# A two-layer transformer trunk on one core: down weights of the experts asked for from a second queue, tokens in residue order, gate product first

## The chip, the core and the metric

One NeuronCore of a Trainium2 chip runs the whole program. Its engines are TensorE (PE in the profile; PEld is its weight load), VectorE (DVE), ScalarE (ACT), GpSimd (POOL) and SyncE (SP). Each has its own instruction stream and they wait for each other on semaphores. Sixteen DMA engines move data between HBM and the on-chip memory (SBUF); here SP and GpSimd ask for transfers, each on its own queue. Products are accumulated in PSUM, which has 8 banks of 128 x 512 floats. The metric is the time of one execution on the device, in microseconds (us).

## What is computed

256 tokens of width 1024 go through two layers. Each layer has four token mixers in parallel, a feed-forward part (dense in layer 0, top-2 of 8 experts in layer 1), and a gated input embedding.

```python
def dilated_attention(q, k, v, window, dilation):      # mixer C: (128, 1), (512, 4), (2048, 16)
    # positions t = u*d + c are split into d residue classes, each a sliding window
    o, lse = banded_attention(to_classes(q), to_classes(k), to_classes(v), window // (2 * dilation), C_BLOCK, None)
...
    merged = merged + gates[:, :, n] * (o.reshape(bsz, seq, BRANCH_WIDTH) @ w_branch[n])
...
def swiglu(h, wg, wu, wd):
    return (jax.nn.silu(h @ wg) * (h @ wu)) @ wd
# layer 1: every token goes to 2 of 8 experts, each with wg, wu (1024 x 3584) and wd (3584 x 1024)
    h = rms_norm(x, ffn_pre_g[i]); x = x + rms_norm(f, ffn_post_g[i])
    e = (p[i] @ ple_w_proj[i]) * sigmoid(x @ ple_w_gate[i]); x = x + rms_norm(e, ple_post_g[i])
```

All arrays are float32, and the eight experts' weights are 352 MB of the 507 MB that are read.

## The kernel before

Tokens lie as two tiles of 128: token `t*128 + p` is in partition p of tile t. All large weights pass through `ring`, six slots of 1 MB each. SP asks for them in the order of `ring_plan()`; before a slot is filled again SP waits for the semaphore that tells that its last contents are used (`released`, `expert_load`). A wait on SP holds back everything behind it on SP.

Precise products are made of three rounded ones. ACT casts a weight slot to a rounded copy (`expert_his`, L1370 and L1373, "hi"), DVE subtracts that from the slot (`expert_los`, L1809 and L1814, "lo"), and PE multiplies hi by hi, hi by lo and lo by hi.

**The experts.** `expert_chunk` is written once for each engine and runs 56 times, for 8 experts of 7 chunks of 512 hidden columns. A chunk b uses six loads: slots 0 and 1 (two halves of the up weights), 2 and 3 (gate), 4 and 5 (down). PE's order in a chunk is: up product with slot 0; the transposition of the hidden values of chunk b-1 (`expert_turn`, L983, here called the turn); up product with slot 1; the down product of chunk b-1 (L964, slots 4 and 5); gate products with slots 2 and 3 (all of them L1022). In one chunk of each expert PE also gathers the next expert's tokens (L974), and in another it scatters the last expert's result (L1003). ACT's order is: casts of slots 0 and 1 of b, cast of slot 4 of b-1, silu of b-1 (L1378), cast of slot 5 of b-1, cast of the turned hidden values (L1382), casts of slots 2 and 3, and a copy of the up product out of PSUM (L1432). DVE's is: splits of slots 0 and 1 of b, split of slot 4 of b-1, the multiplication of silu by up (`expert_hidden`, L1821), split of slot 5 of b-1, split of the turned values (L1825), splits of slots 2 and 3. Slots 0 to 3 come free when PE has used them (`up_gate_used`), 4 and 5 when DVE has split them (`down_split`). SP asks in the order 0 and 1 of b, 4 and 5 of b-1, 2 and 3 of b. The rows of up and gate weights in a slot are 2 KB long, those of down weights 4 KB.

**The mixers.** `MIXER` is one list of steps that each engine follows. PE does for each head: two `fill` units (L1170, L1177), `turn` (transposed probabilities, L1140), `score` of the next head (L909) and `pv` (L1153). Mixer C, the last of the four, has three sets of scores in a head, one for each pair of window and dilation, all 256 keys wide, in banks 4 and 5; the third one follows `pv`. One exponential runs over all sets together.

**The start.** SP asks for x in two tiles, a small table, four weight loads and then the tables (1.5 MB). DVE waits for both tiles of x, and splits the first weights after the first tile of x is transposed.

Of the kernel before, what the change touches and what calls it, by code (L numbers as in the profile page):

```python
# [27 lines left out]
ALU = mybir.AluOpType  # L28
# [35 lines left out]
                ("mask", 4 * NT * SEQ), ("full", 2 * NT * HD), ("axial", 2 * NT * HD), ("rope_a", 2 * NT * A_ROPE))  # L64
# [4 lines left out]
CONST_W = _n  # L69


def constants():
# [12 lines left out]
    q = (np.arange(NT)[None, :] * P + p[:, None])[:, :, None]  # L85
    k = np.arange(SEQ)[None, None, :]
    masks = []
    for window, dil in PATTERNS:
        masks.append((q % dil == k % dil) & (np.abs(q - k) <= window // 2))
    masks.append(np.abs(q - k) <= D_HALF_WINDOW)  # L90
# [9 lines left out]
    pos = np.arange(NT)[None, :] * P + p[:, None]  # L100
# [52 lines left out]
NSETS = {"A": 1, "B": 1, "C": 3, "D": 1}  # L153
# [113 lines left out]
class ExpertPass:  # L267
# [3 lines left out]
    def __init__(self, sem, tag, slots, loads0):  # L271
# [4 lines left out]
        self.up_copied, self.silu_ready = sem(f"{tag}_up_copied"), sem(f"{tag}_silu_ready")  # L276
# [69 lines left out]
def trunk(nc, args):  # L346
# [5 lines left out]
    with ctx:  # L352
# [44 lines left out]
        peak = sb("peak", [P, 2, NT, 3])  # L397
# [21 lines left out]
        probs = take(2 * NT * 3 * SEQ).rearrange("p (j t g s) -> p j t g s", j=2, t=NT, g=3)  # L419
# [32 lines left out]
        e_hidden, e_silu, e_up = hidden[:, 0:ECW], silu[:, 0:ECW], silu[:, ECW:2 * ECW]  # L452
# [38 lines left out]
        UP_BANK, TURN_BANK, GATE_BANK, SPREAD_BANK = (ps[:, b, :] for b in range(4))  # L491
# [10 lines left out]
        mask = const("mask", 4 * NT * SEQ).rearrange("p (m t s) -> p m t s", m=4, t=NT)  # L502
# [4 lines left out]

        const_in_s, x_in_s = sem("const_loaded"), [sem(f"x{t}_loaded") for t in range(NT)]
# [27 lines left out]
        main_pass = ExpertPass(sem, "moe", slot_in, [(LOOPS[1] + j) // RING for j in range(RING)])  # L536
# [27 lines left out]
        def loaded(eng, pos):  # L564

            eng.wait_ge(slot_in[pos % RING], 16 * (pos // RING + 1))
# [22 lines left out]
        def _(sp):  # L589
# [74 lines left out]
            def all_expert_loads(run):  # L664

                def chunk(b, e, c, before):
                    for j in (0, 1):
                        expert_load(run, j, b, e, c)
                    if before:
                        for j in (4, 5):  # L670
                            expert_load(run, j, b - 1, *before)
# [3 lines left out]
                for j in range(RING):  # L675
                    expert_load(run, j, 0, 0, 0)
# [7 lines left out]
                for j in (4, 5):  # L684
                    expert_load(run, j, ALL_CHUNKS - 1, N_EXPERTS - 1, E_CHUNKS - 1)
# [5 lines left out]
            expert_views = [moe_view(moe_w_up[0]), moe_view(moe_w_gate[0]),  # L691
                            moe_w_down[0].rearrange("e (c h k p) d -> e c h p k d", h=2, k=2, p=P)]

            x_v, first = x_in[0].rearrange("(t p) d -> p t d", p=P), CONST_AT["upper"]
# [1383 lines left out]
```

## Time and profile before

| | before |
|---|---|
| median of 3 runs | 2068.84 us (2068.57 to 2075.63) |
| the profiled execution | 2068.97 us, of which the span is 2067.2 us |
| PE busy, PEld busy | 1985.2 us (96%), 1677.5 us (81%) |
| DVE, ACT, POOL busy | 1355.1 us, 1106.8 us, 58.6 us |
| bytes by SP's queue, by GpSimd's | 497.92 MB, 7.91 MB |
| experts (first gather to last scatter) | 997.55 to 2015.6 us of the span |

The span is what the profiler sees of the program. Times within it count from its start. PE is busy nearly always, but a busy PE says little on a whole, since its ends are modelled; the distance between the starts of its groups is the better measure. The page's DMA row for the experts shows 324 to 374 GB/s in each slice, against 102 to 194 in most of the rest.

### The profile page before, as it was taken

The numbers are of one execution on the slowest core, as the hardware profiler recorded it, in microseconds if no ns is written. First come the engines' busy times: TensorE is split into PE (matmuls) and PEld (weight loads), VectorE is DVE, ScalarE is ACT, GpSimd is POOL, SyncE is SP. The second block draws the span as 40 slices with busy tenths as digits, with TensorE's granted clock in tenths as the row PEclk, the third lists the DMA queues.
The fourth block names the chain that finished last, engine by engine and source line by source line (L and its number), as shares of the span: only waits on it lengthen the run. The fifth ranks groups of instructions, "written<-read, shape, count | busy, mean of one in ns | idle before, by whom it ended". The sixth has DMA issues, their size and how long they took to land.

```text
span 2067.2 us, 27265 instructions
## 1 busy us (share of the span) xinstructions
PE 1985.2 (96%) x10126; PEld 1677.5 (81%) x10126; DVE 1355.1 (66%) x1504; ACT 1106.8 (54%) x1174; POOL 58.6 (3%) x104
## 2 busy tenths in 40 slices
PE   6999998999998999999799999999999999999986
PEld 5888887999986888887688888878888888888864
DVE  3345345555546424435588888888888888888864
ACT  4233334333335333333477776777777777777743
POOL 2100002000001100000000000000000000000000
PEclk9999999999999999999799999999999999999998
DMA  8533336555535533323599998999999999998970
GB/s 299 163 102 103 102 122 190 188 187 187 188 133 194 189 118 102 123 91 132 220 368 342 353 372 325 374 331 354 359 338 374 338 356 350 351 373 324 374 288 28
DMA packets 253345, 506.70 MB, mean 245 GB/s; under 512 B 8304, under 2 KB 90384, under 8 KB 253152
## 3 DMA queue, kind: packets, MB, share of 16 engines
q1 hardware_dynamic: 250592, 497.92, 67.1%
q0 software_dynamic: 2688, 7.91, 1.3%
q8 instruction: 42, 0.69, 0.1%
q14 instruction: 23, 0.19, 0.0%
HBM read 504.75 MB, written 1.05 MB: 245 GB/s over the span
## 4 chain that ended last, share of the span: by engine, by line
PE 89%; DVE 3%; ACT 3%; DMA 2%; issue 2%; SPq 0%; POOL 0%; DVEq 0%; ACTq 0%; POOLq 0%
PE ps L1022 27%; PE ps L964 19%; PE ps L1170 11%; PE ps L934 9%; PE ps L866 4%; PE ps L1109 4%; PE ps L1177 3%; PE ps L909 2%; PE ps L844 2%; PE ps L974 2%; PE ps L1153 1%; DMA ring<-in_w_in_dram 1%; PE ps L983 1%; PE ps L1140 1%; ACT down_hi_w L1373 1%
## 5 line engine op out<-in xcount | busy, mean ns | idle before, releaser
L1809 DVE TENSOR_TENSOR ring_lo<-ring,up_gate_hi_w 128x2048 fp32r<-128x2048 f32 x224 | 504.4, 2289 | 62.5 <-ACT up_gate_hi_w L1370 61.6
L1370 ACT CAST up_gate_hi_w<-ring 128x2048 fp32r<-128x2048 f32 x224 | 423.5, 1914 | 86.3 <-DMA ring<-in_moe_w_up_dram 82.5
L1022 PE MATMUL ps<-up_gate_hi_w,tokens_hi 128*128 128x512 f32 x896 | 355.1, 396 | 1.3 <-DVE ring_lo L1809 1.3
L1022 PE MATMUL ps<-up_gate_hi_w,tokens_lo 128*128 128x512 f32 x896 | 349.5, 390 | 0.0
L1022 PE MATMUL ps<-ring_lo,tokens_hi 128*128 128x512 f32 x896 | 349.0, 389 | 0.0
L1814 DVE TENSOR_TENSOR down_lo_w<-ring,down_hi_w 128x2048 fp32r<-128x2048 f32 x112 | 256.6, 2291 | 56.8 <-ACT down_hi_w L1373 56.4
L1170 PE MATMUL ps<-hT,ring 128*128 128x256 f32 x1024 | 231.7, 379 | 0.0
L1373 ACT CAST down_hi_w<-ring 128x2048 fp32r<-128x2048 f32 x112 | 214.1, 1912 | 25.2 <-DMA ring<-in_moe_w_down_dram 24.2
L1170 PEld LDWEIGHTS ps<-hT,ring 128*128 128x128 f32 x1024 | 193.5, 190 | 26.1 <-issue 0.3
L1022 PEld LDWEIGHTS ps<-up_gate_hi_w,tokens_lo 128*128 128x128 f32 x896 | 168.2, 188 | 35.9
L1022 PEld LDWEIGHTS ps<-up_gate_hi_w,tokens_hi 128*128 128x128 f32 x896 | 168.3, 188 | 35.2 <-issue 1.7
L1022 PEld LDWEIGHTS ps<-ring_lo,tokens_hi 128*128 128x128 f32 x896 | 168.4, 188 | 33.2
L964 PE MATMUL ps<-down_hi_w,hidden_hi 128*128 128x512 f32 x576 | 181.7, 397 | 3.4 <-DVE hidden_lo L1825 3.3
L964 PE MATMUL ps<-down_lo_w,hidden_hi 128*128 128x512 f32 x576 | 179.0, 392 | 0.0
L964 PE MATMUL ps<-down_hi_w,hidden_lo 128*128 128x512 f32 x576 | 178.2, 391 | 0.0
L934 PE MATMUL ps<-hT_hi,up_gate_hi_w 128*128 128x256 f32 x512 | 146.0, 285 | 1.4 <-DVE hT_lo L1630 1.4
L934 PE MATMUL ps<-hT_hi,ring_lo 128*128 128x256 f32 x512 | 145.9, 285 | 0.0
L934 PE MATMUL ps<-hT_lo,up_gate_hi_w 128*128 128x256 f32 x512 | 145.9, 285 | 0.0
L964 PEld LDWEIGHTS ps<-down_lo_w,hidden_hi 128*128 128x128 f32 x576 | 108.7, 189 | 23.6
L964 PEld LDWEIGHTS ps<-down_hi_w,hidden_lo 128*128 128x128 f32 x576 | 108.6, 189 | 23.5
L964 PEld LDWEIGHTS ps<-down_hi_w,hidden_hi 128*128 128x128 f32 x576 | 103.3, 189 | 29.3 <-issue 8.3
L1517 ACT ACTIVATE egate<-ps 128x256 f32<-128x256 f32 x64 | 24.6, 385 | 179.0 <-PE ps L1177 179.0
(218 smaller groups left out, 2661.0 us busy)
## 6 DMA issues: line engine op xcount, KB each, us to landing
ring<-in_moe_w_up_dram SPq DMA_DIRECT2D x112, 1024.0 KB, 5.0
ring<-in_moe_w_gate_dram SPq DMA_DIRECT2D x112, 1024.0 KB, 5.0
ring<-in_moe_w_down_dram SPq DMA_DIRECT2D x112, 1024.0 KB, 8.6
ring<-in_w_in_dram SPq DMA_DIRECT2D x58, 1024.0 KB, 5.2
ring<-in_ffn_w_up_dram SPq DMA_DIRECT2D x16, 1024.0 KB, 5.3
ring<-in_ffn_w_gate_dram SPq DMA_DIRECT2D x16, 1024.0 KB, 7.9
ring<-in_ffn_w_down_dram SPq DMA_DIRECT2D x16, 1024.0 KB, 9.6
ring<-in_w_branch_dram SPq DMA_DIRECT2D x8, 1024.0 KB, 4.9
```

Source lines behind the costliest of these rows:

```text
L844: m = mm(bank[:, 0:w], a[:, 4 * half + k, t * P:(t + 1) * P], b[:, k, 0:w], start=(half == k == n == 0), stop=(half == 1 and k == 3 and n ...
L866: m = mm(acc(t)[:, half, :], a[:, 2 * i + k, t * P:(t + 1) * P], w[:, k, half * 512:(half + 1) * 512], start=(i == k == n == 0), stop=(i = ...
L934: m = mm(ps[:, j, i * SEQ:(i + 1) * SEQ], w[:, k, cols], xs[:, k, :], start=(k == 0 and n == 0), stop=(k == NK - 1 and n == 2))
L964: m = mm(to(t)[:, half, :], a[:, j, t * P:(t + 1) * P], w[:, j % 2, half * 512:(half + 1) * 512], start=first and n == 0, stop=last and n ...
L1022: m = mm(bank, xs[:, 4 * half + k, :], w[:, k, :], start=(half == k == n == 0), stop=(half == 1 and k == 3 and n == 2))
L1109: m = mm(bank[:, t * SEQ:(t + 1) * SEQ], hT[:, k, t * P:(t + 1) * P], wv[:, k, :], start=(k == 0), stop=(k == NK - 1))
L1170: mm(bank[:, 0:SEQ], wg[:, k, (c % 2) * P:(c % 2 + 1) * P], hT[:, k, :], start=(k == 0), stop=(k == NK - 1))
L1177: m = mm(bank[:, SEQ:2 * SEQ], wb[:, k, c * P:(c + 1) * P], oT[:, 2 * n + k, :], start=(k == 0), stop=(k == 1))
L1370: copy(up_gate_hi_w[:, j, :], ring[:, slot, :]).then_inc(run.up_gate_hi, 1)
L1373: copy(down_hi_w[:, j - 4, :], ring[:, slot, :]).then_inc(run.down_hi, 1)
L1809: v.tensor_tensor(ring_lo[:, slot, :], ring[:, slot, :], up_gate_hi_w[:, j, :], ALU.subtract)\
L1814: v.tensor_tensor(down_lo_w[:, j - 4, :], ring[:, slot, :], down_hi_w[:, j - 4, :], ALU.subtract)\
```

## The change

It has four parts.

1. **Down weights on GpSimd's queue.** In the experts of layer 1 slots 4 and 5 are asked for by GpSimd (`down_load`), which waits on `down_split` itself; SP asks only for slots 0 to 3. These two slots get semaphores of their own.
2. **Gate first.** The gate weights take slots 0 and 1 and the up weights 2 and 3. ACT makes silu at the end of its chunk, the copy of the up product is gone, and DVE multiplies straight out of PSUM.
3. **Residue order.** Token `4*(p % 64) + 2*t + p // 64` is in partition p of tile t, so that tokens of one tile agree mod 4 only with tokens of the same tile. In mixer C the sets for dilation 4 and 16 need the keys of their own tile alone and share one set: NSETS of C goes from 3 to 2. x, p and the output are moved in halves of 64 partitions, and the mask table is 256 KB smaller.
4. **Early weights.** At the start the first weight load stands ahead of the second tile of x, ACT casts and DVE splits it before the second tile's work, and the tables have their own semaphore.

```diff
+            def down_load(j, e, c):
+                slot = expert_slot(j)
+                dst = ring[:, slot, :].rearrange("p (k c) -> p k c", k=2)
+                pool.dma_start(dst, down_view[e][c][j % 2]).then_inc(main_pass.slots[slot], 16)
...
+                if layer % 2:
...
+                    with pool.Fori(1, N_EXPERTS) as e:
+                        with pool.Fori(0, E_CHUNKS) as chunk:
+                            for j in (4, 5):
+                                pool.wait_ge(main_pass.down_split, 2 * (e * E_CHUNKS + chunk - 1) + j - 3)
+                                down_load(j, e, chunk)
...
-                    if before:
+                    if before and run is over_pass:
                         for j in (4, 5):
                             expert_load(run, j, b - 1, *before)
...
-                    wait_from(pe, run.up_copied, b)
-                    product(UP_BANK, 0)
+                    wait_from(pe, run.silu_ready, b)
+                    product(GATE_BANK, 0)
...
-                    product(GATE_BANK, 2)
-                    product(GATE_BANK, 3)
+                    wait_from(pe, run.hidden_ready, b)
+                    product(UP_BANK, 2)
+                    product(UP_BANK, 3)
...
-                act.wait_ge(run.up_gate_used, 4 * b + 4)
+                act.wait_ge(run.up_gate_used, 4 * b + 2)
...
-                dve.wait_ge(run.up_copied, b + 1)
+                dve.wait_ge(run.up_gate_used, 4 * b + 4)
                 wait_from(dve, run.turned, b)
-                v.tensor_tensor(e_hidden, e_silu, e_up, ALU.mult).then_inc(run.hidden_ready, 1)
+                v.tensor_tensor(e_hidden, e_silu, UP_BANK, ALU.mult).then_inc(run.hidden_ready, 1)
...
+                    if g == 0:
+                        q, k = score_operands(b, h, 0)
+                        m = mm(bank[:, t * SEQ:(t + 1) * SEQ], q[:, tile], k, start=True, stop=True)
+                        continue
+                    for i in range(2):
+                        q, k = score_operands(b, h, 1 + i)
+                        m = mm(bank[:, t * SEQ + i * P:t * SEQ + (i + 1) * P], q[:, tile], k[:, tile], start=True, stop=True)
...
-                    for t in range(NT):
-                        act.wait_ge(x_in_s[t], 16)
-                        square((layer, "pre", t), x[:, t, :], junk)
+                    act.wait_ge(x_in_s[0], 32)
+                    square((layer, "pre", 0), x[:, 0, :], junk)
+                    z_his(layer, 0, 0)
                     tile_his(layer, "pre", 0)
```

The loads of a later chunk on SP, in the loop over the chunks of the first expert. Before, `ring` is filled with up, up, down, down, gate, gate, and the down loads stand behind the wait for the second up slot:

```order
L662 ISA [waits moe_up_gate_used]
L662 DMA ring<-in_moe_w_up_dram 128x4x512
L657 REGISTER_ALU
L662 ISA [waits moe_up_gate_used]
L662 DMA ring<-in_moe_w_up_dram 128x4x512
L659 ISA
L662 ISA [waits moe_down_split]
L662 DMA ring<-in_moe_w_down_dram 128x2x1024
L659 REGISTER_ALU
L662 ISA [waits moe_down_split]
L662 DMA ring<-in_moe_w_down_dram 128x2x1024
```

The same loop after, on SP; gate stands where up stood, and no down load is left:

```order
L673 ISA [waits moe_up_gate_used]
L673 DMA ring<-in_moe_w_gate_dram 128x4x512
L668 REGISTER_ALU
L673 ISA [waits moe_up_gate_used]
L673 DMA ring<-in_moe_w_gate_dram 128x4x512
L668 REGISTER_ALU
L673 DMA ring<-in_moe_w_up_dram 128x4x512 [waits moe_up_gate_used]
L668 REGISTER_ALU
L673 DMA ring<-in_moe_w_up_dram 128x4x512 [waits moe_up_gate_used]
```

And on GpSimd, where after the load of p nothing but the down loads stands until the experts are done:

```order
L827 DMA work<-in_p_dram 64x2x256 [waits residual_ready,mix_ready]
L827 DMA work<-in_p_dram 64x2x256
L786 DMA ring<-in_moe_w_down_dram 128x2x1024 [waits mix_ready] x2
L832 UNCONDITIONAL_BRANCH
L832 ISA
L786 ISA [waits moe_down_split]
L786 DMA ring<-in_moe_w_down_dram 128x2x1024
L834 REGISTER_ALU
L786 ISA [waits moe_down_split]
L786 DMA ring<-in_moe_w_down_dram 128x2x1024
```

What moved: a down load no longer stands behind a wait for PE on its queue; it is asked for as soon as DVE has split the slot.

PE in the mixer C of layer 0 before, one head, from its fill units (L1170, L1177) over the transposed probabilities (L1140), scores (L909) and the products with v (L1153):

```order
L1170 MATMUL ps<-hT,ring 128x256 x8
L1177 MATMUL ps<-work,ring 128x256 x2
L1140 MATMUL ps<-cn,work 128x128 x12
L909 MATMUL ps<-work 128x256 x4
L1153 MATMUL ps<-work 64x128 x12
L909 MATMUL ps<-work 128x256 x2
```

The same head after (L1207 and L1214 are the fill units, L1180 the transpositions, L949 and L953 the scores, L1194 the products with v):

```order
L1207 MATMUL ps<-hT,ring 128x256 x8
L1214 MATMUL ps<-work,ring 128x256 x2
L1180 MATMUL ps<-cn,work 128x128 x8
L949 MATMUL ps<-work 128x256 x2
L953 MATMUL ps<-work 128x128 x4
L1194 MATMUL ps<-work 64x128 x8
```

Four transpositions and four products with v are gone; four wide score products became four of 128 columns, and none stands behind the products with v any more.

## Rows read from the trace of the kernel before

**Rows 1.** The page: shares of the chain that ended last.

```profile
PE 89%; DVE 3%; ACT 3%; DMA 2%; issue 2%; SPq 0%; POOL 0%; DVEq 0%; ACTq 0%; POOLq 0%
```

**Rows 2.** Stretches of time: length, busy time and count by engine, PE clock, DMA share, GB/s.

```profile
990.00:1000.00 10.00, 4.75 (x21) 4.65 (x22) 8.27 (x28) 0.38 (x2) 0.00 (x0) 0.50 0.07 29
...
1015.00:1020.00 5.00, 3.12 (x13) 2.17 (x12) 4.46 (x3) 4.97 (x4) 0.00 (x0) 1.00 0.93 352
...
1065.00:1082.00 17.00, 17.00 (x78) 13.95 (x77) 15.61 (x9) 12.97 (x10) 0.00 (x0) 1.00 1.02 375
```

**Rows 3.** PE's timeline, a head of mixer C: start, duration, engine, line, tiles, count.

```profile
244.04 1.47 PE L1140 MATMUL ps<-cn,work 128*128 128x128 f32 x12
245.35 1.89 PE L909 MATMUL ps<-work 128*128 128x256 f32 x8
247.17 1.53 PE L1153 MATMUL ps<-work 128*64 128x128 f32 x24
248.63 1.13 PE L909 MATMUL ps<-work 128*128 128x256 f32 x4
249.60 0.59 PE L1170 MATMUL ps<-hT,ring 128*128 128x256 f32 x2
```

**Rows 4.** The same timeline, two heads with one set.

```profile
183.37 1.03 PE L909 MATMUL ps<-work 128*128 128x256 f32 x4
184.32 0.66 PE L1153 MATMUL ps<-work 128*64 128x128 f32 x8
...
217.55 0.66 PE L1153 MATMUL ps<-work 128*64 128x128 f32 x8 [0.67 <-ACT work L1504]
```

**Rows 5.** The chain in order of time: the gather of 16 products with 128 columns.

```profile
1235.60 3.57 PE ps L974 x32
```

**Rows 6.** Timelines of PE, ACT, DVE and SP, one chunk of the third expert.

```profile
1306.41 0.60 PE L983 MATMUL ps<-cn,work 128*128 128x128 f32 x4
...
1323.26 0.60 PE L983 MATMUL ps<-cn,work 128*128 128x128 f32 x4
...
1314.99 1.92 ACT L1370 CAST up_gate_hi_w<-ring 128x2048 fp32r<-128x2048 f32 x1 [1.28 <-DMA ring<-in_moe_w_up_dram]
1317.64 1.92 ACT L1373 CAST down_hi_w<-ring 128x2048 fp32r<-128x2048 f32 x1 [0.73 <-DMA ring<-in_moe_w_down_dram]
...
1302.84 2.29 DVE L1814 TENSOR_TENSOR down_lo_w<-ring,down_hi_w 128x2048 fp32r<-128x2048 f32 x1 [0.46 <-ACT down_hi_w L1373]
...
1319.70 2.29 DVE L1814 TENSOR_TENSOR down_lo_w<-ring,down_hi_w 128x2048 fp32r<-128x2048 f32 x1 [0.46 <-ACT down_hi_w L1373]
1321.91 0.68 DVE L1821 TENSOR_TENSOR work<-work 128x512 f32<-128x512 f32 x1
...
1306.81 3.51 SPq L662 DMA_DIRECT2D ring<-in_moe_w_up_dram  x2
1310.69 1.00 SPq L662 DMA_DIRECT2D ring<-in_moe_w_down_dram  x2
```

**Rows 7.** The page, DMA issues: KB each, median us from issue to landing.

```profile
ring<-in_moe_w_up_dram SPq DMA_DIRECT2D x112, 1024.0 KB, 5.0
...
ring<-in_moe_w_down_dram SPq DMA_DIRECT2D x112, 1024.0 KB, 8.6
```

**Rows 8.** DMA packets of 987 to 989 us by queue: packets, MB, share of 16 engines.

```profile
q1 hardware_dynamic: 101, 0.41, 55.4%
q0 software_dynamic: 101, 0.35, 44.0%
```

**Rows 9.** DMA packets of two stretches, 1295 to 1298 us and 1299 to 1301 us.

```profile
DMA packets 539, 1.20 MB, mean 401 GB/s; under 512 B 16, under 2 KB 16, under 8 KB 539
...
DMA packets 221, 0.84 MB, mean 420 GB/s; under 512 B 16, under 2 KB 16, under 8 KB 221
```

**Rows 10.** The chain in order of time, at the start: start, us, what.

```profile
10.10 26.26 DMA ring<-in_w_in_dram
...
40.81 11.15 PE ps L844 x48
```

**Rows 11.** PE's timeline at the end of the experts.

```profile
1996.63 0.39 PE L1022 MATMUL ps<-up_gate_hi_w,tokens_lo 128*128 128x512 f32 x1
1998.43 0.66 PE L983 MATMUL ps<-cn,work 128*128 128x128 f32 x4 [1.42 <-DVE work L1821]
2002.42 1.22 PE L964 MATMUL ps<-down_hi_w,hidden_hi 128*128 128x512 f32 x2 [3.33 <-DVE hidden_lo L1825]
```

More of the change, by code:

```diff
@@ L84, in constants @@
     put("iota8", np.broadcast_to(np.tile(np.arange(8, dtype=np.float32), NT), (P, NT * 8)))
[L85 to L90, printed above, removed]
+    pos = token_at()
+    q, k = pos[:, :, None], pos.T.reshape(1, 1, SEQ)
+    near = lambda a, b, window, dil: (a % dil == b % dil) & (np.abs(a - b) <= window // 2)
+    own = pos.T[None, :, :]
+    masks = [near(q, k, *PATTERNS[0]), np.concatenate([near(q, own, *PATTERNS[1]), near(q, own, *PATTERNS[2])], -1),
+             np.abs(q - k) <= D_HALF_WINDOW]
     put("mask", np.stack([np.where(m, 0.0, MASKED) for m in masks], 1).astype(np.float32))
@@ L451, in trunk @@
         silu = take(4 * SEQ)
-        e_hidden, e_silu, e_up = hidden[:, 0:ECW], silu[:, 0:ECW], silu[:, ECW:2 * ECW]
+        e_hidden, e_silu = hidden[:, 0:ECW], silu[:, 0:ECW]
         hidden = hidden.rearrange("p (n s) -> p n s", n=2)
@@ L673, in chunk @@
                         expert_load(run, j, b, e, c)
-                for j in range(RING):
+                for j in range(RING if run is over_pass else 4):
                     expert_load(run, j, 0, 0, 0)
@@ L701, in _ @@
                     load(pos)
+                    if pos == 0:
+                        for c in range(2):
+                            sp.dma_start(x[64 * c:64 * c + 64, 1, :], x_v[c, 1]).then_inc(x_in_s[1], 16)
                     if pos == 3:
-                        sp.dma_start(cn[:, first:], const_in[:, first:]).then_inc(const_in_s, 16)
+                        sp.dma_start(cn[:, first:], const_in[:, first:]).then_inc(tables_in, 16)
                 if layer % 2 == 0:
@@ L1128, in _ @@
                             emptied(layer, "swap", {"A": "Ak", "B": "Bk", "C": "C2k", "D": "Dk"}[b], 1 if b == "A" else 0)
-                        later = MIXER[step_number + 1][0] == "pv" and NSETS[b] == 3
-                        for g in range(2 if later else NSETS[b]):
+                        for g in range(NSETS[b]):
                             score(layer, j, b, h, g)
@@ L1150, in _ @@
                             n = SETS * layer + SET0[j] + g
-                            for kt in range(NT):
+                            for i in range(2):
                                 for t in range(NT):
-                                    m = mm(O_BANK[t * HD:(t + 1) * HD, h % 2, :], values(b, h, g, kt),
-                                           pT[:, n % NPT, kt, t * P:(t + 1) * P],
-                                           start=(g == 0 and kt == 0), stop=(g == NSETS[b] - 1 and kt == NT - 1))
+                                    v = values(b, h, 0, i) if g == 0 else values(b, h, 1 + i, t)
+                                    m = mm(O_BANK[t * HD:(t + 1) * HD, h % 2, :], v, pT[:, n % NPT, i, t * P:(t + 1) * P],
+                                           start=(g == i == 0), stop=(g == NSETS[b] - 1 and i == 1))
                             m.then_inc(pv_done, 1)
-                        before = MIXER[step_number - 1]
-                        if before[0] == "score" and NSETS[before[2]] == 3:
-                            score(layer, *before[1:], 2)
                     elif s[0] == "fill":
```

96 lines of the change are left out of this document (55 added, 41 removed).

## The prediction

> **What bounds the kernel now.** I read the chain that ended last first: PE holds 89% of it, DMA 2% [rows 1]. Then the stretches, to see whether that holds in each stage. In a middle stretch of the experts PE is busy 17.00 of 17.00 us, the clock is 1.00, and the DMA engines move 375 GB/s at a share of 1.02 [rows 2]. So PE is the bound there and the DMA engines are close behind; the reader should see both full at once. The third view is the timelines of a single chunk, because a mean can't tell how much slack a load has. The turn of a chunk starts at 1306.41 us and that of the next at 1323.26, 16.85 us later [rows 6], and it is the same in the other chunks without a gather or scatter. 56 chunks make nearly half of the span, so each 0.1 us in a chunk is 5.6 us.
>
> **Slack of a chunk's loads.** The turn can only start when DVE has multiplied silu by up. DVE does that behind its split of slot 4, which is behind its split of slot 1. The row of the split starts at 1319.70 and takes 2.29, the multiplication takes 0.68 and ends at 1322.6; the turn starts at 1323.26 [rows 6]. That is 0.7 us of slack. The load of slot 1 landed at 1314.98, when ACT's wait for it ended: it was asked for at 1309.95 (the second of the pair that begins at 1306.81 and lasts 3.51, less some 0.37 for its own issue), so it took 5.0 us, which is also the median [rows 6, 7]. From that landing to the end of the multiplication lie at least a cast 1.92, the cast of slot 4 1.92, its split 2.29 and 0.68, together 6.8 us. From the turn to the next request for slot 1 lie 1309.95 - 1306.41 = 3.5 us. So slot 1 runs a loop of L + 10.3 us, where L is its time to landing. With L = 5.0 it is 15.3 and PE's own 16.85 decides; from L = 6.5 on the load decides.
>
> **Part 1, down weights on GpSimd's queue.** What it removes is SP's order, up first and down behind it. DVE ends the split of slot 4 at 1302.84 + 2.29 = 1305.13, but SP asked for the new down weights only at 1310.69, after both up loads [rows 6]. Now GpSimd asks for slot 4 at 1305.2 and for slot 5 some 3 us later, so the down loads are in flight before and beside slot 0 (1306.8) and slot 1 (1309.95). They aren't needed early: before, with 8.6 us to landing, ACT waited 0.73 us for one and PE for none [rows 6, 7].
>
> How two busy queues share the engines is in the trace at one place with packets of 4 KB on both: from 987 to 989 us each queue had 101 packets [rows 8]. They take turns packet by packet. Alone, a 2 KB packet costs an engine 3 us x 16 / 539 = 0.089 us, a 4 KB packet 2 us x 16 / 221 = 0.145 us [rows 9]. A gate or up slot is 512 packets, 32 for an engine; a down slot is 256, 16 for an engine. In turns, a pair takes 0.234 us and SP's queue gets one third of the bytes. Alone slot 1 streams for 32 x 0.089 = 2.85 us, so 5.0 holds 2.15 of fixed time.
>
> Now one chunk, with t = 0 at the turn and w the time by which PE has come to wait for it. Slot 4 is asked for at -0.7, slot 0 at -w, slot 5 at 2.3, slot 1 at 3.5. Take w = 1.2. Slot 0 has 6 packets done when slot 4 starts; 16 pairs end at 3.0 with slot 0 at 22; slot 5 follows at once, 16 pairs end at 6.8, and slot 1 has 6 of its 32. The other 26 take 2.3 us, to 9.1. L is 9.1 - 3.5 + 2.15 = 7.8, the loop 18.1, and w = 18.1 - 16.85 = 1.25: that repeats itself. In the first chunk, with w = 0, the gate slots asked for before are still in transfer and L comes to 9.4, a loop of 19.7 and w = 2.9. Between 1.25 and 2.9 I take 1.5 us, near the value that repeats itself, since w can also swing from chunk to chunk: 56 x 1.5 = **+84 us**. The ends are 56 x 1.25 = 70, and 56 x 2.2 = 123 for halfway to the first chunk's. The gather and scatter lie behind slot 1's product and not in the loop, so they cover little. What is queued behind the late split on DVE is slot 5 and the turned values; on PE everything. The clock held 1.00 from 1015 to 1020 us with PE idle for 1.9 of 5 us, and was 0.50 from 990 to 1000 with it idle for more than half [rows 2]; a gap of 1.5 us in 18 is nearer to the first, so I add nothing for it.
>
> The Trainium skill, DMA: Bandwidth & Descriptors, Queues, rings and completion order, says that each engine takes turns between the rows it has work for and drains a whole packet, typically 9 to 17 descriptors, before it switches. The same page (Rules for kernel authors) says that spreading DMAs over issuing engines gains no bandwidth and only saves issue time. The row of equal counts agrees with the turns; by the second rule alone part 1 would be worth nothing, which is rival C.
>
> **Part 2, gate first.** ACT loses a copy of 0.6 us in a chunk and silu moves ahead; neither is in the loop above (casts, split, multiplication), and PE never waited for them in a middle chunk: 0, up to -0.4 us for each expert where the tokens change. At the end there is a gain. PE stands from 1996.86 to the turn at 1998.43 and again to the down product at 2002.42 [rows 11]. With silu made, the multiplication follows the product at once (0.7 us less), and the split of slot 5 is then no longer behind ACT's late cast (1.1 less): **-1.8**. It would be up to 2.4 more if the clock no longer dropped there.
>
> **Part 3, residue order.** A head of C costs PE, by the starts of its groups, 1.31 (transpositions) + 1.82 + 0.97 (scores) + 1.46 (v) = 5.56 us [rows 3]. After: 8 of 12 transpositions 0.87; 8 of 12 products with v 0.97; one set of wide scores 0.95 [rows 4]; and four score products of 128 columns, for which the nearest row is the gather, 3.57 / 16 = 0.223 each, 0.89 [rows 5]. Sum 3.68, 1.88 less. Should the narrow ones cost as much as wide ones (0.43), it is 1.05 less. Eight heads: -15.0. DVE's and ACT's shorter softmax is off the path. What is late next: in the last head of C nothing lies between transpositions and products with v, and where only 4 transpositions stand there PE waits 0.7 us for ACT's copy [rows 4]; 8 cover 0.4 of that less than 12 did, two layers: +0.8. Together **-14.2**, bounds -7.6 and -15.
>
> **Part 4, early weights.** ACT and DVE treat the first weights earlier and PE could start some 2 us sooner. But PE's chain at the start is a DMA: the fifth weight load, asked for at 10.10, lands 26.26 us later, and PE goes on at 40.81 [rows 10]. The queue is full until then, so all that counts is its bytes: 256 KB of masks less at some 380 GB/s, **-0.7**. Bounds 0 and -2. x and p in halves: two issues of 0.4 us more, hidden but for about 0.2 at the last store.
>
> **Sum.** 2068.97 - 14.2 - 0.7 - 1.8 + 84 = 2136.3, say 2136 us. It is made against the profiled execution, 2068.97, which is the median of 2068.84 for any purpose here.
>
> **The rivals.**
> A, the forecast: the two queues collide and slot 1 decides each chunk. For: equal packet counts, 1.5 us between L = 5.0 and 6.5, a release order that puts both down loads ahead. Against: one place only shows two busy queues, and not with 1 MB loads. 2119 to 2175.
> B, the collision is milder, because loads fall into step or the shares come out nearer to equal bytes: 0.4 us in a chunk, 22 us, 2076.
> C, faster: no harm from the second queue. The mechanism would be that down loads, asked for 5 us earlier, use time in which the DMA engines wait for requests, and L of slot 1 stays under 6.5. It decides if the down loads are through before slot 1 is asked for. Then only parts 2 to 4 are left: 2068.97 - 16.7 = 2052. Against: two down slots alone are 4.6 us of transfer from 1305.2 on, slot 5 is only asked for at about 1308.
> D, GpSimd's requests are late: it makes its descriptors itself, and if a down load took 3 us longer before its first byte it would be late for ACT too, and every split behind it. Over 2175.
>
> **Chances.** A 0.72, B 0.08, C 0.16, D 0.04. The range has to leave out C and D at most, 0.20, so it reaches from 2072 to 2175. A measurement can tell about 0.5%, 10 us, from no change. Faster by more than that is C: 0.16. Within it is B's greater part: 0.08 with the mildest of A. Slower 0.76.
>
> **What would show it.** In the profile after: time to landing of gate loads near 7 to 8 us instead of 5.0 while down loads come in under 8.6; a distance between turns of about 18 us; PE waiting for DVE's multiplication before the turn in most chunks; GB/s in the experts near 325; a head of C shorter by 1.9 us; PE still going on at about 40 us at the start. It is wrong if turns stay 16.85 us apart, and then the sharing of the engines, not the loop, is the step that failed. If the landing of slot 1 is late and the turns are not, the loop is wrong.

## The result, and the profile after

The changed kernel takes 2185.1 us, the median of four runs (2178.9 to 2188.1), against 2068.7 for the kernel before in the same comparison: a ratio of 1.055, 95% interval 1.052 to 1.058. It is slower, as forecast, but by 116 us and not by 67, and outside the forecast's range, which ended at 2175. Of the runs, the profiled one took 2178.91 us, with a span of 2177.2.

Three parts of the page after answer to [rows 1] and [rows 7]: the shares of the chain that ended last by engine, with the start of the groups, ACT's casts (L1407) and their idle time; and the DMA issues with KB and median us to landing.

```profile
PE 65%; DMA 15%; DVE 7%; issue 5%; ACT 5%; SPq 1%; POOL 0%; DVEq 0%; ACTq 0%; POOLq 0%
...
L1407 ACT CAST up_gate_hi_w<-ring 128x2048 fp32r<-128x2048 f32 x224 | 422.3, 1910 | 269.3 <-DMA ring<-in_moe_w_gate_dram 264.7
...
ring<-in_moe_w_gate_dram SPq DMA_DIRECT2D x112, 1024.0 KB, 6.8
ring<-in_moe_w_up_dram SPq DMA_DIRECT2D x112, 1024.0 KB, 5.1
ring<-in_moe_w_down_dram POOLq DMA_DIRECT2D x112, 1024.0 KB, 7.1
```

DMA held 2% of the chain before and holds 15% now; ACT waits 264.7 us for gate loads alone. The loads that are late are the gate's, which SP asks for where it asked for the up loads before; the down loads, which were moved, come in sooner (7.1 for 8.6). The 6.8 is a median over both gate slots: slot 0 alone has 5.2, slot 1 alone 8.7. The windows that answer to [rows 2], with the columns of that group, the third one placed on the start of a chunk:

```profile
1065.00:1082.00 17.00, 16.45 (x74) 13.10 (x73) 11.61 (x7) 8.43 (x7) 1.41 (x2) 1.00 0.99 368
1100.00:1300.00 200.00, 180.69 (x818) 147.25 (x817) 152.53 (x94) 124.30 (x88) 14.04 (x20) 0.97 0.86 312
1430.00:1435.00 5.00, 3.90 (x13) 3.29 (x14) 4.18 (x5) 2.75 (x3) 1.41 (x2) 0.66 0.80 281
```

The DMA engines now move 312 GB/s. The same 200 us of the kernel with parts 2 to 4 alone show 347 and a full PE (below). Nothing was short of bandwidth, then: the loads come in bunches with pauses between; from 1484 to 1486 us, for one, no packet moves at all.

One turn of the loop, from the changed kernel's chain in order of time (start, us, what). It starts at the request for slot 1, 3.54 us after the turn at 1451.97:

```profile
1455.51 9.70 DMA ring<-in_moe_w_gate_dram
...
1467.04 1.91 ACT down_hi_w L1410
...
1469.38 1.44 DVE down_lo_w L1848
...
1471.58 0.69 DVE work L1855
...
1472.39 1.11 PE ps L1027 x4
```

Slot 1 takes 9.70 us to land (L), and from there to the turn at 1472.39 lie 7.18. The distance between these turns is 20.42 us, where [rows 6] has 16.85. The next one, to 1491.27, is 18.88. In the middle chunks of each expert it goes on like that, 19.5 to 21.6 us and 17.4 to 19.6 in turn, and an expert of seven chunks takes 141 us where there were 124.8. The last chunk of an expert, in which PE gathers, takes 20.9 us as before (20.8), but the one behind it takes 21.6 where there were 17.3.

The cheaper places came out as forecast. A head of mixer C on PE, which answers to [rows 3] and [rows 5], by transpositions, wide scores, narrow scores, products with v, and what follows:

```profile
242.23 1.04 PE L1180 MATMUL ps<-cn,work 128*128 128x128 f32 x8
243.10 1.03 PE L949 MATMUL ps<-work 128*128 128x256 f32 x4
243.97 1.05 PE L953 MATMUL ps<-work 128*128 128x128 f32 x8
244.95 1.09 PE L1194 MATMUL ps<-work 128*64 128x128 f32 x16
245.98 3.72 PE L1207 MATMUL ps<-hT,ring 128*128 128x256 f32 x16
```

242.23 to 245.98 is 3.75 us, where the sum had 3.68 and the kernel before 5.56. The end of the experts, which answers to [rows 11]:

```profile
2106.95 0.39 PE L1066 MATMUL ps<-up_gate_hi_w,tokens_lo 128*128 128x512 f32 x1
2108.17 0.66 PE L1027 MATMUL ps<-cn,work 128*128 128x128 f32 x4 [0.84 <-DVE work L1855]
2110.97 1.22 PE L1008 MATMUL ps<-down_hi_w,hidden_hi 128*128 128x512 f32 x2 [2.15 <-DVE hidden_lo L1859]
```

From the last product to the down product it is 4.02 us against 5.79: the 1.8 of part 2.

### The profile page after: what moved, and what is told of

Its sections match the earlier page's. It is cut to its first block, busy times and chain, and to the rows that moved or that the text cites. A ratio compares the mean times of both kernels' runs of the same rounds, so it can differ in the third digit from the quotient of the medians.

```text
span 2177.2 us, 27049 instructions
## 1 busy us (share of the span) xinstructions
PE 2005.6 (92%) x10030; PEld 1685.6 (77%) x10030; DVE 1341.7 (62%) x1472; ACT 1060.0 (49%) x1110; POOL 137.5 (6%) x218
## 4 chain that ended last, share of the span: by engine, by line
PE 65%; DMA 15%; DVE 7%; issue 5%; ACT 5%; SPq 1%; POOL 0%; DVEq 0%; ACTq 0%; POOLq 0%
PE ps L1066 15%; DMA ring<-in_moe_w_gate_dram 14%; PE ps L1207 10%; PE ps L1008 10%; PE ps L978 9%; PE ps L904 4%; PE ps L1151 4%; DVE down_lo_w L1848 3%; ACT down_hi_w L1410 3%; PE ps L1214 3%; PE ps L882 2%; PE ps L1027 2%; PE ps L949 1%; DVE work L1855 1%; DMA ring<-in_w_in_dram 1%
## 5 line engine op out<-in xcount | busy, mean ns | idle before, releaser
L1407 ACT CAST up_gate_hi_w<-ring 128x2048 fp32r<-128x2048 f32 x224 | 422.3, 1910 | 269.3 <-DMA ring<-in_moe_w_gate_dram 264.7
L1066 PE MATMUL ps<-up_gate_hi_w,tokens_hi 128*128 128x512 f32 x896 | 366.1, 409 | 9.2 <-DVE ring_lo L1843 8.5
L1066 PE MATMUL ps<-ring_lo,tokens_hi 128*128 128x512 f32 x896 | 357.4, 399 | 0.0
L1066 PE MATMUL ps<-up_gate_hi_w,tokens_lo 128*128 128x512 f32 x896 | 355.8, 397 | 0.0
L1207 PE MATMUL ps<-hT,ring 128*128 128x256 f32 x1024 | 232.3, 380 | 0.0
L1207 PEld LDWEIGHTS ps<-hT,ring 128*128 128x128 f32 x1024 | 192.8, 190 | 26.7 <-issue 1.4
L1066 PEld LDWEIGHTS ps<-up_gate_hi_w,tokens_hi 128*128 128x128 f32 x896 | 174.1, 194 | 50.1 <-DVE ring_lo L1843 11.3
L1410 ACT CAST down_hi_w<-ring 128x2048 fp32r<-128x2048 f32 x112 | 208.8, 1908 | 1.6 <-DMA ring<-in_moe_w_down_dram 1.6
L1066 PEld LDWEIGHTS ps<-up_gate_hi_w,tokens_lo 128*128 128x128 f32 x896 | 173.4, 194 | 38.0
L1066 PEld LDWEIGHTS ps<-ring_lo,tokens_hi 128*128 128x128 f32 x896 | 173.7, 194 | 34.1
L786 POOL DMA_DIRECT2D ring<-in_moe_w_down_dram x112 | 78.7, 703 | 1044.8 <-DVE down_lo_w L1848 1024.9
```

Source lines behind the costliest of these rows:

```text
L786: pool.dma_start(dst, down_view[e][c][j % 2]).then_inc(main_pass.slots[slot], 16)
L1066: m = mm(bank, xs[:, 4 * half + k, :], w[:, k, :], start=(half == k == n == 0), stop=(half == 1 and k == 3 and n == 2))
L1207: mm(bank[:, 0:SEQ], wg[:, k, (c % 2) * P:(c % 2 + 1) * P], hT[:, k, :], start=(k == 0), stop=(k == NK - 1))
L1407: copy(up_gate_hi_w[:, j, :], ring[:, slot, :]).then_inc(run.up_gate_hi, 1)
L1410: copy(down_hi_w[:, j - 4, :], ring[:, slot, :]).then_inc(run.down_hi, 1)
```

## The experiments

Two theories stood against each other for the loss. Theory 1: the two queues take turns, and that delays slot 1. Theory 2: what delays slot 1 are the bytes asked for ahead of it, whatever the queue. A third, that GpSimd's requests are late by themselves, is rival D. Where a result has no range, it is one execution; the kernel before took 2067 to 2074 us beside all of them.

**Part 1 undone.** Down loads back on SP, as before; the lines with GpSimd's loads are gone and SP's order has no condition:

```
-                    if before and run is over_pass:
+                    if before:
                         for j in (4, 5):
                             expert_load(run, j, b - 1, *before)
```

> The changed kernel with part 1 undone: the down loads are back on SP's queue, behind gate slots 0 and 1 as before. Parts 2, 3 and 4 stay. If the second queue's early requests are the whole loss, in whatever way, this is 2068.9 - 14.2 - 1.8 + 1.1 (the start of the profile after is some 1.1 us later, not 0.7 earlier) = 2054 us, turns 16.85 us apart. If gate first has a part in the loss (the other theory for it), the turns stay over 17.5 us apart and it is over 2090 us.

Measured: 2054.9 us (2052.3 to 2056.3), ratio to the kernel before 0.9925, interval 0.9905 to 0.9944. Its window beside that of the changed kernel:

```profile
1065.00:1082.00 17.00, 17.00 (x78) 14.09 (x77) 14.87 (x9) 12.54 (x9) 0.00 (x0) 1.00 1.02 376
1100.00:1300.00 200.00, 198.69 (x922) 163.70 (x921) 171.94 (x105) 139.95 (x99) 0.00 (x0) 1.00 0.95 347
```

PE is full again and the middle turns are 16.8 us apart, as expected. Part 1 costs 130 us; the other three parts gain 13.4.

**Part 1 alone**, on the kernel before; the lines are those of part 1 in the diff above.

> The kernel before with part 1 alone: down loads asked for by GpSimd as soon as DVE has split the last ones. If part 1 is all of the loss: 2185 + 13 + 2 = 2200 us, turns of some 18 and 21 us. If gate first carries a share of it, it is under 2170 us.

Measured: 2209.6 us, 141 over the kernel before. Gate first carries no part of the loss. With the other three parts in place part 1 loses 11 us less; why is open, and this run is a single execution.

**GpSimd held back.** The line is added in both loops over chunks; this is the second:

```
+                                pool.wait_ge(main_pass.up_gate_used, 4 * (e * E_CHUNKS + chunk) + 2)
                                 pool.wait_ge(main_pass.down_split, 2 * (e * E_CHUNKS + chunk - 1) + j - 3)
```

> The changed kernel, but GpSimd also waits until PE has released slot 1 before it asks for the down weights, so that both queues get their requests in the order in which SP alone had them before. Theory 1, the taking of turns between two queues is what delays slot 1: it now shares from its first packet with slot 4, 16 pairs at 0.234 us and 16 packets at 0.089 and 2.15 fixed, L = 7.3 us, a loop of 17.6, 0.8 us in a chunk, 2054 + 45 = 2099 us. Theory 2, the bytes asked for ahead of slot 1 are what delays it, whatever the queue: these are gone, 2054 us. Theory 3, GpSimd's requests are late by themselves: ACT waits for the down slots and the time stays over 2120 us.

Measured: 2056.0 us, as with part 1 undone. The DMA issues between 1424.8 and 1426.6 us, one chunk's slot 1 and both down loads behind it, and behind them the packets of 1427.1 to 1429 us by queue, which are all SP's (q1; GpSimd's is q0):

```profile
ring<-in_moe_w_down_dram POOLq DMA_DIRECT2D x2, 1024.0 KB, 8.8
ring<-in_moe_w_gate_dram SPq DMA_DIRECT2D x1, 1024.0 KB, 5.0
...
q1 hardware_dynamic: 369, 0.76, 103.5%
```

112 down loads by GpSimd cost nothing if the first of a pair is asked for 0.65 us behind slot 1. That ends rival D, and it speaks for theory 2. It doesn't settle the turns: GpSimd's first packet of slot 4 comes at 1429.1 us, 3.5 us after its request, when slot 1's are nearly through (the last one at 1429.6).

**One queue, early down loads.** The kernel without part 1, with SP's order changed:

```
                     for j in (0, 1):
+                        if before:
+                            expert_load(run, 4 + j, b - 1, *before)
                         expert_load(run, j, b, e, c)
```

> Down loads on SP's queue again, but each ahead of a gate load: slot 4, slot 0, slot 5, slot 1, then the up loads. The times of the requests are near those of the changed kernel, the queue is one. Theory 1, turns between two queues do the harm: no second queue, so it is under 2100 us. Theory 2, the order does it: slot 1 is the last of four loads of 1 MB that are asked for within 5 us, and ends no sooner in one queue than in two: -0.7 + 2 x 2.32 + 2 x 2.85 = 9.6, L = 8.3 us, a loop of 18.6, near the changed kernel's time: 2160 to 2200 us.

Measured: 2203.4 us, with one queue, 3 over the range expected by theory 2. A second queue isn't needed for the loss. Landings of one chunk, each added up from request and L: slot 4 at 1486.4, slot 0 at 1489.1, slot 5 at 1491.7, slot 1 at 1494.4. A megabyte takes 2.6 to 2.7 us and they come one behind the other.

**Slot 4 early only**, slot 5 behind slot 1, one queue.

```
+                    if before:
+                        expert_load(run, 4, b - 1, *before)
                     for j in (0, 1):
                         expert_load(run, j, b, e, c)
                     if before:
-                        for j in (4, 5):
-                            expert_load(run, j, b - 1, *before)
+                        expert_load(run, 5, b - 1, *before)
```

> One queue as in the run with early down loads on SP, but only slot 4 is asked for ahead of slot 0; slot 5 comes behind slot 1. Theory 2, slot 1 lands when all loads asked for ahead of it are through: slot 4 is asked for 0.5 us before the turn, lands 4.85 us later, slots 0 and 1 follow at 2.7 us each, so slot 1 lands 9.7 us after the turn and the next turn is 7.2 later: 16.9, PE's own 16.85. So 2054 to 2060 us although half of the down bytes are early. If harm goes with the bytes that are early (the rival), half of 131 us is left: 2120 us.

Measured: 2118.8 us, 64 over the kernel with parts 2 to 4. The number is the rival's, so this expectation failed. By the medians slot 1 is asked for 3.6 us after the turn and lands 7.2 later, at 10.8 and not 9.7, and with 7.2 behind it that is 18.0 from turn to turn; the middle turns are 17.1 to 19.1 us apart. One early load is enough to pass the slack; my landing time was 1.1 us too early, and 56 chunks make that 60 us. The loop with the right landing and the rival's share of the bytes come to nearly the same number, so this run doesn't part them.

**Slot 0 first.** One queue: slot 0, both down loads, slot 1.

```
-                    for j in (0, 1):
-                        expert_load(run, j, b, e, c)
+                    expert_load(run, 0, b, e, c)
                     if before:
                         for j in (4, 5):
                             expert_load(run, j, b - 1, *before)
-                    for j in (2, 3):
+                    for j in (1, 2, 3):
```

> One queue: slot 0, slot 4, slot 5, slot 1, then the up loads. Theory 2, with slot 0 asked for as soon as PE has released it, w before the turn, where PE waits w: the string of four loads starts at -w instead of -0.5, slot 1 lands at -w + 5.0 + 3 x 2.65 = 12.95 - w, the loop is 20.15 - w, and with w = loop - 16.85 it is 18.5: 1.65 us in a chunk, 2054 + 56 x 1.65 = 2146 us, against 19.6 in the run with slot 4 first. The rival, it is only the count of loads ahead of slot 1: as there, 2200 us.

Measured: 2195.9 us. That is near the rival's number. The fixed point that I had worked out again, the distance at which the loop repeats itself (18.5), doesn't hold as a mean: the middle turns are 20.3 to 20.8 and 17.9 to 19.6 us apart in turn, 19.7 on average. SP's own timeline shows both kinds of chunk (start, us from the first to the last of a pair, count):

```profile
1761.37 0.37 SPq L669 DMA_DIRECT2D ring<-in_moe_w_gate_dram  x1
1764.20 3.08 SPq L669 DMA_DIRECT2D ring<-in_moe_w_down_dram  x2
1769.85 0.37 SPq L669 DMA_DIRECT2D ring<-in_moe_w_gate_dram  x1
...
1783.54 0.38 SPq L669 DMA_DIRECT2D ring<-in_moe_w_gate_dram  x1
1784.29 1.00 SPq L669 DMA_DIRECT2D ring<-in_moe_w_down_dram  x2
1786.66 0.37 SPq L669 DMA_DIRECT2D ring<-in_moe_w_gate_dram  x1
```

Where PE has waited, the turn is at 1764.68, slot 0 was asked for 3.3 us earlier, the four requests spread over 8.5 us, and slot 1 lands after 5.0. PE doesn't wait for the next turn. Then nothing is spread: four requests in 3.1 us, slot 1 after 10.1, and the turn behind it comes 20.8 us after this one. PE's timeline at the turn of 1764.68, behind such a wait, and the clock of the 5 us:

```profile
1764.68 0.92 PE L1001 MATMUL ps<-cn,work 128*128 128x128 f32 x4 [3.54 <-DVE work L1829]
1765.25 0.78 PE L1040 MATMUL ps<-up_gate_hi_w,tokens_hi 128*128 128x512 f32 x1
1765.82 0.63 PE L1040 MATMUL ps<-ring_lo,tokens_hi 128*128 128x512 f32 x1
1766.25 0.63 PE L1040 MATMUL ps<-up_gate_hi_w,tokens_lo 128*128 128x512 f32 x1
...
1764.00:1769.00 5.00, 4.32 (x14) 3.58 (x15) 4.30 (x4) 3.37 (x3) 0.00 (x0) 0.66 0.99 377
```

The products start 0.43 us apart and not 0.23: the clock is at its lower level, 1.2 GHz, for the first seven or so. So the short chunk is not 16.85 us either. It is PE's own 16.85 and 1.6 for the clock, 18.45.

**PE kept busy.**

```
+                wait_from(pe, run.turned_split, b)
+                for j in range(12):
+                    nc.tensor.transpose(TURN_BANK[:, j % 4 * P:(j % 4 + 1) * P], ident, ident)
                 pe.wait_ge(run.hidden_ready, b + 1)
-                wait_from(pe, run.turned_split, b)
```

> The changed kernel, with 12 transpositions of the identity (about 1.3 us) on PE ahead of each turn, in the time in which it waits for DVE; their result is overwritten. If the clock's fall to half after a wait has a part in the loss (up to 1.5 us from the turn to the next request for slot 1 in every second chunk), the clock stays nearer to 1.00 and the time falls by 54 x 0.5 = 27 us to 2158 although PE does more. Theory 2 says that a later request for slot 1 is answered sooner by as much, since the loads ahead of it end when they end: no gain, and where a wait is shorter than 1.3 us a loss, 2183 to 2200 us.

Measured: 2165.7 us, 19 less than the median of the changed kernel and 13 less than the fastest of its four executions, although PE does 1.5 us more in each chunk. PE's timeline at one wait, the filler (L1026) and the turn behind it (L1029):

```profile
1466.32 1.47 PE L1026 MATMUL ps<-cn 128*128 128x128 f32 x12
...
1468.45 0.65 PE L1029 MATMUL ps<-cn,work 128*128 128x128 f32 x4 [0.66 <-DVE work L1857]
```

Of the wait only 0.66 us is left idle, and the four transpositions of the turn take 0.65 and not 1.11; the mean clock is 0.983, against 0.971. The expectation that a late request costs nothing has fallen. The changed kernel's own trace shows why. Here are two of its waits of the same length with the turn behind each short chunk, and the windows of 5 us at the two waits; after the first the clock stays at 1.00, after the second it is at 0.67:

```profile
1332.62 0.65 PE L1027 MATMUL ps<-cn,work 128*128 128x128 f32 x4 [2.52 <-DVE work L1855]
1350.01 0.65 PE L1027 MATMUL ps<-cn,work 128*128 128x128 f32 x4 [0.38 <-DVE work L1855]
...
1472.39 1.11 PE L1027 MATMUL ps<-cn,work 128*128 128x128 f32 x4 [2.51 <-DVE work L1855]
1491.27 0.54 PE L1027 MATMUL ps<-cn,work 128*128 128x128 f32 x3 [0.50 <-DVE work L1855]
...
1332.00:1337.00 5.00, 4.38 (x21) 3.69 (x22) 4.55 (x4) 3.69 (x3) 1.41 (x2) 1.00 0.99 376
1472.00:1477.00 5.00, 4.61 (x17) 3.88 (x17) 4.11 (x4) 3.47 (x3) 1.41 (x2) 0.67 1.01 388
```

Slot 1 is asked for 3.6 and 4.9 us after the turn, since PE releases it later at the lower clock, and lands 6.6 and 6.8 us after its request: the later request isn't answered sooner. So the short chunk takes 17.4 us in one case and 18.9 in the other, and the clock's 1.4 to 1.5 us count in full. In the changed kernel slot 1 is asked for that late in 14 of 53 chunks, in this run in 4.

**Parts 2 and 3 alone.** Part 1 is undone, and of part 4 the order of the first loads and of ACT's and DVE's first work; the tables keep their own semaphore.

> Parts 2 and 3 alone: down loads on SP in the old order, and the start of the old kernel (both halves of x ahead of the weights, ACT and DVE treat x before the first weights). If early weights are worth anything it is slower than the kernel with parts 2 to 4: by 2 us at most; if x's late second half costs 1.1 us, it is that much faster. 2053 to 2057 us, a difference that the comparison can hardly tell; what it tells is in the trace: the time of the first product with v, 98.8 to 99.6 us without part 4 and 98.9 to 100.4 with it so far.

Measured: 2058.6 us (2055.9 to 2062.1), where 2053 to 2057 were expected; ratio 0.9945, interval 0.9929 to 0.9962, which overlaps with that of parts 2 to 4. The first product with v starts at 101.4 us here and at 98.8 and 99.6 in the two other traces without part 4; in the ten traces with it at 98.8 to 100.9. Part 4 is worth nothing that these runs can show.

**The turn sooner.** The loop can also be shortened on DVE. In the changed kernel:

```
+                        expert_hidden(run, b - 1)
                         expert_los(run, b - 1, 4)
-                        expert_hidden(run, b - 1)
...
+                        turned_los(run, b - 1)
                         expert_los(run, b - 1, 5)
-                        turned_los(run, b - 1)
```

> The changed kernel, down loads early on GpSimd's queue as they are, but DVE multiplies silu by up ahead of its split of slot 4, and treats the turned values ahead of its split of slot 5. In the changed kernel 7.2 us lie between slot 1's landing and the turn: cast 1.9, splits of slot 1 and slot 4 2.2 each, multiplication 0.6 and 0.1. Without the split of slot 4 it is 5.0, so slot 1 may take L = 16.85 - 3.55 - 5.0 = 8.3 us instead of 6.1 before PE waits. DVE also splits slot 4 later, so GpSimd asks 2.2 us later for it: slot 0 lands 5.0 after the turn, slot 4 at 7.7, slot 1 at 10.3, L = 6.8. By the theory of the loop nothing is late then: 2052 to 2070 us. The rival, the DMA engines have no room for early down loads whatever DVE's order (a lack of bandwidth): it stays over 2140 us.

Measured: 2111.2 us (2108.6 to 2126.6), ratio 1.023, interval 1.018 to 1.027. From slot 1's landing to the turn it is 5.0 us now, as expected, and 74 us are won, but the time is 41 us over the range expected, because L went up, to a median of 9.1 (8.7 in the changed kernel), and not down to 6.8. Since DVE splits slots 4 and 5 later, their requests moved as well: by the medians slot 0 is asked for 0.3 us before the turn, slot 4 2.8 after it, slot 1 at 3.6 and slot 5 at 5.5, where the changed kernel had slots 4 and 5 both ahead of slot 1. The 74 us are the worth of the shorter path and of that order together. The DMA issues of one chunk, slot 4 (1483.94) with slot 1 (1484.75), then slot 5 (1486.69); behind them the packets of 1491 to 1492 us by queue, with MB and their time as a share:

```profile
ring<-in_moe_w_down_dram POOLq DMA_DIRECT2D x1, 1024.0 KB, 5.3
ring<-in_moe_w_gate_dram SPq DMA_DIRECT2D x1, 1024.0 KB, 8.6
...
ring<-in_moe_w_down_dram POOLq DMA_DIRECT2D x1, 1024.0 KB, 7.8
...
q0 software_dynamic: 65, 0.27, 67.1%
q1 hardware_dynamic: 66, 0.13, 35.0%
```

Slot 4 lands at 1489.2. With 2.65 us a megabyte slot 1 should land at 1491.9; it lands at 1493.35, since slot 5, asked for 1.9 us later on the other queue, takes part. Its first packet comes at 1490.6, when slot 1's have been moving since 1488.6. Packet for packet GpSimd's 4 KB get two thirds of the time. This is the turn-taking of [rows 8], with 1 MB loads. A lack of bandwidth, the rival, doesn't fit the 74 us.

**The same order, one queue.** DVE's new order, and SP asks for slot 0, slot 4, slot 1, slot 5.

```
                     expert_load(run, 0, b, e, c)
                     if before:
                         expert_load(run, 4, b - 1, *before)
                     expert_load(run, 1, b, e, c)
                     if before:
                         expert_load(run, 5, b - 1, *before)
```

> DVE's new order as in the run before, but the down loads on SP's queue, in the order in which that run's requests went out: slot 0, slot 4, slot 1, slot 5, then the up loads. There, on two queues, slot 4 landed 5.3 us after its request, slot 1 8.6 and slot 5 7.8, though slot 5 was asked for 1.9 us after slot 1: both shared the engines from the landing of slot 4 on. Theory 1 in its narrower form, a later request on the other queue takes time from slot 1: on one queue slot 1 ends before slot 5 begins, at 5.0 + 2 x 2.65 = 10.3 us after the turn, L = 6.8, under 8.3, no wait, 2048 to 2058 us. Theory 2 alone, it is only what is asked for ahead of slot 1, whatever the queue: L stays near 9 and the time near the 2111 of that run, over 2095.

Measured: 2049.3 us (2048.3 to 2055.2), ratio 0.991, interval 0.989 to 0.993. One chunk's slot 1, asked for at 1470.32, and slot 5, 0.8 us behind it:

```profile
ring<-in_moe_w_gate_dram SPq DMA_DIRECT2D x1, 1024.0 KB, 7.3
...
ring<-in_moe_w_down_dram SPq DMA_DIRECT2D x1, 1024.0 KB, 9.0
```

One load ahead and one behind, as in the run before, and the one behind is asked for even sooner; L has a median of 7.3 and not 9.1, and the loss is gone. So both theories hold, each in its place. What is asked for ahead of slot 1 delays it on any queue (theory 2). What is asked for behind it did not delay it on its own queue, and on the other queue it did where slot 1 was still being moved when the later load's first packet came, 3.9 us after its request (theory 1). In the run with GpSimd held back nothing was ahead of slot 1, it was through 4.65 us after its request, and the later loads took nothing from it.

The Trainium skill, DMA: Bandwidth & Descriptors, Rules for kernel authors, says that more issuing engines bring no bandwidth. The traces of these two runs agree (323 to 335 GB/s in stretches of 200 us with two queues, 347 to 355 on one), and show what the rule leaves out: a second queue can cost 62 us at equal order.

**DVE's order on SP's queue**, in the kernel with parts 2 to 4: part 1 undone, and the edit of the run with the turn sooner.

> Parts 2 to 4 with down loads on SP, and DVE's new order. PE has no wait in middle chunks there, so there is nothing to gain but in the chunks around gather and scatter: 2050 to 2056 us, no difference that can be measured from 2054.9. If PE waits for the later split of slot 4 or 5 in its down products it is slower, 2060 us or more.

Measured: 2048.0 us (2047.7 to 2048.4), ratio 0.990, interval 0.988 to 0.992. That is 2 us under the range expected and 1% under the kernel before, the lowest median found; the run before it, 2049.3, can't be told from it. It is 7 us less than with part 1 undone alone. Of that, 1.6 us lie ahead of the first turn and 2.7 in the first expert (105.2 us for 107.9), where PE had waited; a later expert takes 124.4 to 124.6 us, against 124.5 to 124.7 or, in the two in which PE had waited, 125.7 and 126.0.

## Why the prediction was right and wrong

**Right.** It is slower, and by the mechanism that was forecast: the loop of slot 1 and its slack, the down loads' bytes ahead of slot 1 as the cause, and PE waiting before the turn (for more than 0.3 us in 34 of 53 chunks). The gate loads take 6.8 us at the median where 7 to 8 stood (slot 1 alone 8.7), down loads come in under 8.6, and GB/s are down, to 312 where 325 stood. Parts 2 to 4 were to gain 16.7 and gained 13.4. In part 3 a head saves 1.81 us (1.88 forecast); from the first to the last product with v of a layer it comes to 6.9 us, in both layers 13.7 for the 14.2. Part 2 gives its 1.8 at the end of the experts. Part 4 gives nothing where -0.7 stood: PE goes on at 41.94 us at the start, not at 40.81. From the start of the last down product to the end the changed kernel takes 66.2 us for 64.8, where the forecast had 0.2 more; the cause is open. Rival C is excluded. So is D: 2185 us is in the region that D gave, but the run with GpSimd held back excludes its mechanism. (Rival B's 2076 should read 2075, 2052.3 + 22.4.)

**Wrong: the term of +84 us.** It was 130 by the medians, and 122 between the first and the last turn of the two profiled executions. I multiplied 56 by 1.5 us, a value "near the value that repeats itself", and named the swing only as a reason to go a little above it. In 53 chunks of the changed kernel the mean from turn to turn is 20.1 us, against 17.8 before: 2.3 us, just above the 2.2 from which the upper end of the range was made. In the 31 middle chunks, clear of gather and scatter, the mean is 19.38 us: 3.90 from the turn to the request for slot 1, 8.27 for L and 7.21 from the landing to the next turn. The working had 3.5, 7.8 and 6.8. Each of the three was too small by about the same amount, 0.4 to 0.5 us.

First, L and the fixed point. The loop doesn't settle. Behind a long wait the next requests are spread, slot 1 lands in 5.6 to 7.3 us and PE waits for 1.0 us at most; behind that chunk the requests are bunched again. My own first chunk (L of 9.4, loop of 19.7) was the better picture of every second chunk; one of them measured L of 9.7 and 20.4. But the mean of both kinds, 8.27, is only 0.5 above the fixed point's 7.8. The gather covers nothing on the whole: its own chunk loses 0.1 us, and the one behind it 4.3.

Second, the clock. "I add nothing for it" was read off a window of 5 us with 1.9 us idle. Of the 53 chunks, 22 begin with a wait of 2.5 us or more (up to 5.8). Behind 14 of these waits the clock is at its lower level for the first microseconds and slot 1 is asked for 4.9 to 6.2 us after the turn, together 22 us later than at the full clock; behind eight others, of 2.5 to 3.3 us, it stays at the higher level, and these traces don't show what decides. Covering the wait gave back 19 us net of the filler.

Third, the path behind the landing. I took a cast, the cast of slot 4, its split and the multiplication, 6.8 us, and called it "at least". DVE also splits slot 1 in that time, and its two splits in a row decide. DVE's timeline in the turn shown above, splits of slot 1 and slot 4:

```profile
1467.16 2.29 DVE L1843 TENSOR_TENSOR ring_lo<-ring,up_gate_hi_w 128x2048 fp32r<-128x2048 f32 x1 [0.36 <-ACT up_gate_hi_w L1407]
1469.38 2.28 DVE L1848 TENSOR_TENSOR down_lo_w<-ring,down_hi_w 128x2048 fp32r<-128x2048 f32 x1
```

With the cast's 1.9 ahead of them, the multiplication's 0.7 and 0.1 to the turn behind, and 2.2 us from start to start for each split, that is 7.2 us in 29 of the 53 chunks; in the seven behind a gather it is 8.3. By these counts the term is worth some 22 us, an estimate: 29 x 0.4 and 7 x 1.5. The three overlap, since a longer path also makes longer waits, so their shares don't simply add up.

The turn-taking, on which the working spent most of its care, isn't needed for the changed kernel's loss: one queue with both down loads ahead of slot 1 gave 2196 and 2203 us. Nor do the queues always take turns, as the working had it. From 1454 to 1456 us the changed kernel has these packets by queue, though slot 0 was asked for at 1452.37:

```profile
q0 software_dynamic: 199, 0.82, 99.9%
q1 hardware_dynamic: 17, 0.02, 2.6%
```

Slot 4, asked for first, is moved alone; slot 0 and slot 5, both waiting by then, share the engines from 1456 on.

## What to carry to other kernels

Where a load that is needed soon stands behind a chain of engines, count the bytes that are asked for ahead of it and the bytes that another queue has in flight beside it; a slot that came free early is no reason to fill it early. Don't take the value at which a loop with waits repeats itself for its mean: follow two or three rounds, with PE's slower products behind a wait, and put every engine between landing and wait into the sum, not the shortest chain alone. If a load decides, look first at the engine that works in order between its landing and the waiting one: moving the multiplication and one small split each ahead of a large split was worth 74 us of 130 with early down loads, which were then asked for later as well, and 7 us without them.

## What was not expected of the hardware

Where two queues both have packets to move, they share by packets, not by bytes: 65 and 66 packets in one microsecond, 0.27 and 0.13 MB. But a load asked for while the other queue was moving one did not share with it from the start: in the run with GpSimd held back its first packet came 3.5 us after its request, at the end of the other load, in the run with the turn sooner 3.9 us after it, when the other had been moving for 2.0. At one load ahead and one behind, a 1 MB load of 2 KB packets took 9.1 us with the later load, of 4 KB packets, on another queue, and 7.3 with that load on its own queue (medians). And PE was faster with more work: 12 transpositions in each wait took 19 us off 2185 (one execution).
